# The prompt's probabilities turned by VectorE and SBUF copies instead of TensorE transposes, in a two-branch attention layer

## The reference

```python
def _dense_attn(q, k, v):
    s = jnp.einsum('bqhd,bkhd->bhqk', q, k).astype(jnp.float32) * ATTN_SCALE
    p = _softmax_f32(s).astype(v.dtype)
    o = jnp.einsum('bhqk,bkhd->bqhd', p, v)
    return o.reshape(q.shape[0], q.shape[1], -1)
```

## Time and profile before

| | us |
|---|---|
| time, median of 3 runs | 1204.24 |
| the three runs | 1206.59, 1204.24, 1203.47 |
| span of the profiled execution, first to last instruction | 1206.4 |
| TensorE matmul busy | 1182.1 (98%) |
| VectorE busy | 827.8 (69%) |
| ScalarE busy | 610.5 (51%) |
| 928 transposes at line 1165, 64 of them of the prompt | 124.7 busy |

### The profile page before, as it was taken

The page is one execution under the profiler, slowest core; times in us unless marked ns, Lnnn a source line. Parts: engine busy times, 40 slices in busy tenths (PEclk is TensorE's granted clock), DMA queues, the critical chain, the costliest instruction groups (busy, mean ns, idle before and its releaser), DMA issues.

```text
span 1206.4 us, 19639 instructions
## 1 busy us (share of the span) xinstructions
PE 1182.1 (98%) x7384; PEld 1080.7 (90%) x7384; DVE 827.8 (69%) x1621; ACT 610.5 (51%) x1224; POOL 97.0 (8%) x110
## 2 busy tenths in 40 slices
PE   7999999999999999999999999999999999999998
PEld 1899889989998999899899999989989988998996
DVE  6869458756766775687687697688679876354453
ACT  6742335534543554465465555556547675344342
POOL 0000200000000000000000000000000034533431
PEclk9999989999999999999999999999999999999999
DMA  9817612141122213221411111411023376642640
GB/s 360 307 52 227 226 35 68 47 138 46 57 83 93 65 40 103 81 72 65 144 64 40 55 58 46 112 62 58 22 60 120 119 237 204 214 149 91 208 141 35
DMA packets 71362, 132.81 MB, mean 110 GB/s; under 512 B 6758, under 2 KB 48102, under 8 KB 71276
## 3 DMA queue, kind: packets, MB, share of 16 engines
q1 hardware_dynamic: 57452, 109.70, 28.0%
q10 hardware_dynamic: 13824, 21.96, 5.0%
HBM read 96.24 MB, written 35.40 MB: 109 GB/s over the span
## 4 chain that ended last, share of the span: by engine, by line
PE 83%; DVE 8%; ACT 3%; DMA 2%; issue 2%; SPq 1%; POOL 0%; ACTq 0%; DVEq 0%
PE d_ps_pairs L94 23%; PE s_ps_pairs L94 11%; PE y_ps L2043 9%; PE o_ps_pairs L1195 9%; PE b_ps L94 9%; PE t_ps_pairs L1165 8%; PE v_ps L94 4%; PE s_ps_pairs L1129 4%; PE s_ps_pairs L1128 4%; DMA x<-in_w_ada 2%; PE k_ps L415 1%; DVE mn L1565 1%; DVE q L1550 1%; PE v_ps L429 1%; DVE pt L1559 1%
## 5 line engine op out<-in xcount | busy, mean ns | idle before, releaser
L94 PE MATMUL d_ps_pairs<-h,wt 128*128 128x384 f32 (+4 forms) x1848 | 352.1, 345 | 0.9 <-ACT craw L1358 0.9
L94 PEld LDWEIGHTS d_ps_pairs<-h,wt 128*128 128x128 f32 x1848 | 317.9, 188 | 14.7 <-ACT craw L1358 1.9
L1559 DVE TENSOR_TENSOR pt<-t_ps_pairs,pt 128x512 fp32r<-128x512 f32 (+2 forms) x264 | 153.0, 620 | 62.3 <-ACT pt L1313 60.8
L94 PE MATMUL s_ps_pairs<-h,wt 128*128 128x512 f32 (+1 forms) x864 | 174.7, 359 | 3.0 <-DVE q L1516 3.0
L94 PEld LDWEIGHTS s_ps_pairs<-h,wt 128*128 128x128 f32 x864 | 143.4, 191 | 25.2 <-DVE q L1516 3.2
L1313 ACT ACTIVATE pt<-t_ps_pairs 128x512 fp32r<-128x512 f32 (+2 forms) x264 | 130.2, 544 | 25.6 <-PE t_ps_pairs L1165 20.3
L1337 ACT ACTIVATE pr<-s_ps_pairs,mx 128x896 f32<-128x896 f32 (+1 forms) x128 | 124.9, 981 | 27.1 <-DVE mx L1587 26.8
L1165 PE MATMUL t_ps_pairs<-ident_sb,pr 128*128 128x128 f32 x928 | 124.7, 274 | 0.8 <-DVE pt L1559 0.3
L2043 PE MATMUL y_ps<-wo,mg 128*128 128x512 f32 (+1 forms) x504 | 113.2, 385 | 0.0
L1165 PEld LDWEIGHTS t_ps_pairs<-ident_sb,pr 128*128 128x128 f32 x928 | 105.6, 140 | 6.5 <-DVE pt L1559 3.1
L2043 PEld LDWEIGHTS y_ps<-wo,mg 128*128 128x128 f32 x504 | 91.4, 188 | 20.5
(11 more groups left out here) (217 smaller groups left out, 1618.4 us busy)
## 6 DMA issues: line engine op xcount, KB each, us to landing
wraw<-in_w_gate SPq DMA_DIRECT2D x24, 512.0 KB, 3.7
gt<-gates_d SPq DMA_DIRECT2D x40, 256.0 KB, 4.5
v_d<-vst SPq DMA_DIRECT2D x20, 320.0 KB, 4.6
wada<-in_w_ada SPq DMA_DIRECT2D x12, 512.0 KB, 7.1
gates_d<-craw ACTq DMA_DIRECT2D x30, 192.0 KB, 1.9
oz<-gates_d SPq DMA_DIRECT2D x20, 256.0 KB, 4.4
oz<-o_d SPq DMA_DIRECT2D x20, 256.0 KB, 4.1
x_f<-in_x SPq DMA_DIRECT2D x10, 512.0 KB, 6.5
```

The source lines that it names most:

```text
L94: mm = eng.matmul(out, lhs(a, k), rhs(b, k), start=(k == 0 and i == 0), stop=(k == n_k - 1 and i == 2))
L1559: dve.tensor_tensor(pt[:, 1, c * 512:c * 512 + cols], t_ps[:, n % 2, 0:cols], pt[:, 0, c * 512:c * 512 + cols].bitcast(F32), ALU.subtract) ...
```

## The change

In the prompt's step the probabilities are no longer turned by TensorE. VectorE, after the scaling, transposes each of the four 128x256 tiles in squares of 32 by 32 (four instructions), into a new tile `sq` in which squares that go to the same partitions lie together. SyncE then issues sixteen copies from SBUF to SBUF, of 32 partitions by 1 KB each, that bring row group i and column group j of the squares to their places in a new tile `qt`. ScalarE's high halves and VectorE's low halves of the prompt read `qt` where they read `t_ps`. The new waits: VectorE's squares for its own scalings; SyncE's copies for the squares (`sq_done`); ScalarE's high half for all copies (`qt_in`, 16 x 16 per pair); ScalarE's exponentials of step 1, which overwrite `pr`, for the squares. TensorE's eight transposes of the prompt and the wait for the scaling ahead of them are gone. Some semaphores of the two branches are merged to stay within their number, and memory is made for the new tiles.

```diff
@@ pairs: helpers
+    def prompt_squares(t, h):
+        if A:
+            return sq[:, :, :].rearrange("p j (h k t a) -> p h k t j a", h=2, k=2, t=2)[:, h, :, t]
+        return sq[:, :, :].rearrange("p j (k h t a) -> p k h t j a", h=2, k=2, t=2)[:, :, h, t]
+    def turned_prompt(c):
+        return qt[:, :, 4 * c * 32:4 * (c + 1) * 32].rearrange("p i (b a) -> p b i a", a=32)
@@ SyncE, behind the loads of the values
+            sp.wait_ge(sq_done, (pb + 1) * 4)
+            for i in range(4):
+                for j in range(4):
+                    sp.dma_start(qt[32 * j:32 * (j + 1), i, :], sq[32 * i:32 * (i + 1), j, :]).then_inc(qt_in, 16)
             load_tile(1)
@@ TensorE
-                if s > 0:
-                    for c in range(min(2, chunks[s - 1])):
+                if s > 1:
+                    for c in range(2):
                         transposes(s - 1, c)
@@ ScalarE, high
-                    act.wait_ge(t_done, chunk_base(p) + n + 1)
+                    if s == 0:
+                        act.wait_ge(qt_in, (pb + 1) * 256)
+                    else:
+                        act.wait_ge(t_done, turned_count(p, n + 1))
+                    if s == 0:
+                        act.activation(pt[:, 0, c * 512:c * 512 + cols].rearrange("p (b i a) -> p b i a", i=4, a=32),
+                                       turned_prompt(c), ACT.Copy).then_inc(hi_done, 1)
+                        continue
@@ ScalarE, exps
-                        act.wait_ge(t_done, chunk_base(p) + (chunk0[s - 1] + min(2, chunks[s - 1]) if s > 0 else 0))
+                        if s == 1:
+                            act.wait_ge(sq_done, (pb + 1) * 4)
+                        else:
+                            act.wait_ge(t_done, turned_count(p, chunk0[s - 1] + 2 if s > 0 else 0))
@@ VectorE, low
+                    if s == 0:
+                        part = lambda n: pt[:, n, c * 512:c * 512 + cols].rearrange("p (b i a) -> p b i a", i=4, a=32)
+                        dve.tensor_tensor(part(1), turned_prompt(c), part(0).bitcast(F32), ALU.subtract).then_inc(lo_done, 1)
+                        continue
@@ VectorE, normalise
+                if s == 0:
+                    for t, h in ((0, 0), (0, 1), (1, 0), (1, 1)):
+                        c = 2 * t + h
+                        scaled = dve.tensor_scalar(prompt_probs(t, h), prompt_probs(t, h), rden[:, c:c + 1], None, ALU.mult)
+                        if h == 1:
+                            scaled.then_inc(p_done, 1)
+                    dve.wait_ge(p_done, pb * 2 * STEPS + 2)
+                    for t, h in ((0, 0), (0, 1), (1, 0), (1, 1)):
+                        dve.transpose(prompt_squares(t, h),
+                                      prompt_probs(t, h).rearrange("p (k j b) -> p k j b", j=4, b=32)).then_inc(sq_done, 1)
+                    return
@@ kernel
-    nc = bacc.Bacc("TRN2", target_bir_lowering=False, num_devices=1)
+    nc = bacc.Bacc("TRN2", target_bir_lowering=False, num_devices=1, dynamic_dma_scratch_size=1024)
```

More of the change, by code:

```diff
@@ L842, in pairs @@
     s_ps, t_ps, o_ps, d_ps = (tiles[n] for n in ("s_ps", "t_ps", "o_ps", "d_ps"))
+    sq, qt = tiles["sq"], tiles["qt"]
     CH = 2 if A else 1
@@ L884, in pairs @@
     (craw_in, c_split, ckh, cvh, s_done, m_done, exp_done, r_done, p_done, t_done, hi_done, lo_done, pva_done,
-     pvb_done, ot_done, o_done, d_done, g_done) = (counts[n] for n in COUNTS)
+     pvb_done, ot_done, o_done, d_done, g_done, sq_done, qt_in,
+     proj_done, xa, xd, m1_done) = (counts[n] for n in COUNTS)
     g_out = [counts["g_out0"], counts["g_out1"]]
-    proj_done, xa, xd, x_used = sem("proj_done"), sem("xa"), sem("xd"), sem("x_used")
-    vw_in, m1_done, o_out = sem("vw_in"), sem("m1_done"), sem("o_out")
+    vw_in, o_out, x_used = sem("vw_in"), sem("o_out"), sem("x_used")
+    proj0, x0, m10 = (0, 0, 0) if A else (PAIRS * 6, PAIRS * 9, PAIRS * SAMPLES)
     if A:
@@ L919, in chunk_base, with turned_count @@
         return (0 if A else PAIRS * NCHUNK["a"]) + p * NCHUNK[branch]
+    def turned_count(p, n):
+        return chunk_base(p) + n - 2 * (p + base) - (2 if n >= 2 else 0)
+    def prompt_squares(t, h):
[4 more added lines that the diff above has]
+        return qt[:, :, 4 * c * 32:4 * (c + 1) * 32].rearrange("p i (b a) -> p b i a", a=32)
     def rows(ap, g):
@@ L1276, in projected @@
                 tok, bank = slice(t0, t0 + tn), s_ps[:, bank, 0:tn]
-                act.wait_ge(proj_done, p * NG + n + 1)
+                act.wait_ge(proj_done, proj0 + p * NG + n + 1)
                 if A and n < 3:
@@ L1367, in tile_high @@
                 else:
-                    sem, value = [(d_done, UNIT0[pb]), (proj_done, p * NG + 3), (d_done, UNIT0[pb] + ENDS[pb][0]),
+                    sem, value = [(d_done, UNIT0[pb]), (proj_done, proj0 + p * NG + 3), (d_done, UNIT0[pb] + ENDS[pb][0]),
                                   (d_done, UNIT0[pb] + ENDS[pb][1 if last else 2])][n]
@@ L1545, in projected @@
                         dve.tensor_copy(q1[HD:P, h, tok], rot[h * HD:(h + 1) * HD, 0:tn]).then_inc(xd, 1)
-                    dve.wait_ge(xa, p * 6 + 2 * n + 2)
-                    dve.wait_ge(xd, p * 6 + 2 * n + 2)
+                    dve.wait_ge(xa, x0 + p * 6 + 2 * n + 2)
+                    dve.wait_ge(xd, x0 + p * 6 + 2 * n + 2)
                     for h in range(2):
@@ L1573, in minima @@
                     dve.wait_ge(band_in, 16)
-                    dve.wait_ge(m1_done, p * STEPS + s + 1)
+                    dve.wait_ge(m1_done, m10 + p * STEPS + s + 1)
                     dve.tensor_tensor(nm[:, 0:2], mn[:, 0:2], nsk[:, :], ALU.min).then_inc(m3_done, 1)
@@ L1600, in prompt_minima @@
                 dve.tensor_reduce(grid4(mn), both, AX.X, ALU.min).then_inc(m1_done, 1)
-                dve.wait_ge(m1_done, p * STEPS + 1)
+                dve.wait_ge(m1_done, m10 + p * STEPS + 1)
                 dve.wait_ge(nsk_done, p + 2)
@@ L1619, in normalise @@
                 dve.wait_ge(r_done, pb * STEPS + s + 1)
-                for t in range(2):
[L1621 to L1627, removed]
+                if s == 0:
[9 more added lines that the diff above has]
+                    return
+                for t in range(2):
                     dve.tensor_scalar(probs_run(s, t), probs_run(s, t), rden[:, t:t + 1], None, ALU.mult
@@ L2155 @@
 COUNTS = ("craw_in", "c_split", "ckh", "cvh", "s_done", "m_done", "exp_done", "r_done", "p_done", "t_done",
-          "hi_done", "lo_done", "pva_done", "pvb_done", "ot_done", "o_done", "d_done", "g_done")
+          "hi_done", "lo_done", "pva_done", "pvb_done", "ot_done", "o_done", "d_done", "g_done", "sq_done", "qt_in",
+          "proj_done", "xa", "xd", "m1_done")
 TILES_TOTAL = 3 + 5 * PAIRS + 4 * PAIRS
 GAP0, GAP1, GAP2 = 896, 512, 344
+SPARE = 1792
 def build(nc, io):
@@ L2172, in build @@
     with ExitStack() as ctx:
+        turn = {n: sb(ctx, n, shape) for n, shape in (("sq", [P, 4, 8 * 32]), ("qt", [P, 4, 8 * 32]))}
+        sb(ctx, "spare", [P, SPARE])
         hm = sb(ctx, "h", [P, 2, KD, TOK], F32R)
@@ L2207, in build @@
             ("pr", [P, 2, NB + PAST + NB], F32), ("pt", [P, 2, 14 * P], F32R))}
+        tiles.update(turn)
         psum = ExitStack()
@@ L2222, in build @@
     with ExitStack() as ctx:
+        sb(ctx, "turned", [P, 4 * 4 * P + SPARE])
         wb = [wt[:, 0, :, :], wt[:, 1, :, :]] + [sb(ctx, f"wb{j}", [P, 2, D], F32R) for j in range(2, KD)]
```

## The result

The changed kernel takes 1266.79 us (median of 4 runs, 1265.07 to 1268.3), the kernel before in the same series 1204.80 (1203.47 to 1206.59): a ratio of 1.0513, interval 1.0497 to 1.0528. That is 62.0 us slower, where 36.4 had been forecast, and 4.8 us above the range. The direction held; the size is that of rival (b), whose rate of issue was the true one.

The account below looks back on a forecast made before the run. TensorE, busy 98%, was taken to bound the kernel, with VectorE and ScalarE on the chain in B. Delays of 14.4 us in A, 10 for A's clock and 12 in B made 36.4, so 1240.6 us; range 1216 to 1262.

Parts of the forecast that it names:

- rival (b): SyncE's queue backs up at a pitch of 0.60 to 0.70 us; at 0.65, 30 us more, 1270 us; chance 0.12.
- the pitch of SyncE's issues: Sixteen copies in a row on SyncE's queue: 0.40 us each, ends 0.28 and 0.70; last begins 6.0 us after first.
- The landing: Each SBUF-to-SBUF copy: 1.9 us from issue to landing, plus 0.1 for the semaphore.
- The path behind the landing: ScalarE's high halves await all copies, delaying step 1's exponentials and TensorE; in A TensorE stalls 4.1 us.
- the sum for a pair of A: Scores of step 2 start 3.6 us later per pair of branch A, TensorE's gain counted in; 14.4 us over four.
- The clock in A: TensorE's clock falls behind the stall in each pair of A, costing 2.5 us each, 10 us in all.
- Rival (a): The clock holds at 2.4 GHz in the pairs of A: 10 us less, 1230.6 us; chance 0.25.
- The clock in B: A clock fall in B would stretch TensorE to about VectorE's chain: nothing taken, at most 1 us per pair.
- case (c): Issues are cheap, copies land some 2 us behind squares: A gains 3.5, B loses 6, 1206.8 us; chance 0.05.
- Squares: VectorE's four 128x256 square transposes per pair: 1.5 us taken, between 1.1 and 2.9.
- The gain on TensorE: Eight transposes removed per pair: 0.87 us in each pair of A, 3.5 in all; nothing in B.
- case (d): Copies land inside unit 1, in A within 3.6 us of the squares: 7.0 us faster, 1197.2 us; chance 0.03.

Follow-up runs that it names:

- The experiment with eight forms: Changed kernel with a different form of SBUF-to-SBUF copy in each of the eight pairs, to read the issue pitch; one execution, 1249.36 us.
- Eight copies: Changed kernel with eight copies of 64 partitions per pair in place of sixteen of 32, same bytes; 1225.46 us, ratio 1.0169 to the kernel before.
- Two queues: Changed kernel with eight of the sixteen copies issued by SyncE and eight by ScalarE; 1251.07 us, ratio 1.0369 to the kernel before.
- By way of DRAM: Changed kernel with five DMAs per pair instead of sixteen copies: four writes to DRAM, one read back; 1238.19 us, ratio 1.0274 to the kernel before.
- the filler: Changed kernel with unused matmuls behind unit 1 (28 per pair of A, 14 of B) to fill TensorE's stall; 1262.95 us, ratio 1.0477.
- free copies: Changed kernel without the sixteen copies, the halves reading the squares where they lie; 1210.22 us, ratio 1.0041 to the kernel before.
- squares alone: Kernel before plus VectorE's four square transposes per pair, which nobody reads; TensorE's transposes stay, no copies; 1212.13 us, ratio 1.0058.
- the late reading by way of DRAM: Changed kernel with five DMAs through DRAM, and the prompt's halves and weighted sum moved behind step 1's weight split and transposes; 1235.93 us, ratio 1.0254.
- sixteen read late: Changed kernel with its sixteen copies, the prompt's halves and weighted sum moved behind step 1's weight split and transposes; 1252.12 us, ratio 1.0401.

## Why the prediction was wrong

**The step that failed** is the pitch of SyncE's issues: 0.40 us taken, 0.63 measured. It is fifteen pitches in each of eight pairs, 8 x 15 x 0.23 = 27.6 us. The landing, the wait of ScalarE for the last copy and the path behind it came as forecast; the last copy was issued too late. I had rows for two partitions (0.24), for 128 (0.46) and for strided ones (0.70), and placed 32 partitions between the first two by their number of rows. The experiment with eight forms shows that rows don't enter. None of those rows was a series of copies from SBUF to SBUF, and the dearest one, 0.70 (eight in a row, strided; 0.66 to 0.80 over the four pairs of A), I had set aside with "four times the rows". Rival (b) gave 1270 at 0.65; at 0.63 it gives 1268. It deserved far more than 0.12, and the range should have reached to it. (That the queue backs up, as (b) put it, isn't shown: the pitch is the same for 8 KB as for 128 KB.)

**The path behind the landing** was right. TensorE was to stand still for 4.1 us in A, and with the measured pitch for 4.1 + 3.45 = 7.55; it did for 7.62. With the measured pitch the sum for a pair of A is 3.6 + 3.45 = 7.05 us and the clock, for one of B 3.0 + 3.45 = 6.45; B measured 6.4 to 6.5. The three kernels that vary the data's arrival bear out A: 3.6 us less one for each us by which the data comes sooner than 8.0. Eight copies, with the clock held: 2.0 by the sum, 2.4 measured. Two queues: 2.9 and the clock, 5.5 measured. By way of DRAM: 4.1 and the clock, 5.6 measured.

**The clock in A** was right in its mechanism and somewhat too large: 2.5 us taken. What the sum leaves for it is 9.06 - 7.05 = 2.0 in the third pair (1.6 to 2.7 over the four), 2.6 with two queues and 1.5 by way of DRAM; the filler gives 1.4 to 1.9. Four times 0.5 is 2 us less than my sum. With both corrections: 36.4 + 27.6 - 2.0 = 62.0, which is the measured difference; that it fits to the tenth is luck, as the pairs of A differ among themselves by 1 us. Rival (a), that it holds, did not come.

**The clock in B** was taken at nothing. In the changed kernel this holds: the fall lies behind the 4.48 us stall in the second pair and inside unit 1 (6.00 us) in the third, and both intervals are longer by what the arrival of the data explains. With free copies or squares alone it costs 0.9 to 1.4 us, and my price for case (c), 6 us in B, was too low for that reason: 10.

**Squares**: 1.42 us for four, 1.5 taken. **Landing**: 1.9, 1.9 taken. **The gain on TensorE**: 0.87 us in each pair of A by the row, 0.8 to 0.9 in the run with free copies; in B nothing. **Faster**, case (d), asked for data 3.6 us behind the squares; with 6.4 the pair already lost 2.4. Its 1197.2 was out of reach at any pitch: with free copies, which come 0.7 us behind the squares, the kernel takes 1210.2, as B gains nothing from the transposes that go and pays for the squares.

The rule that I set against my rows in case (c), in the Trainium skill's "DMA: Bandwidth & Descriptors", Issuing engines are not separate DMA queues, is that the time to start a DMA is usually small beside the DMA itself. For one copy here it is a third, 0.63 us beside a landing of 1.9; for sixteen in a row it misleads, as 10.06 us of issuing stand beside one landing of 1.9. What the same section says of several engines, that starting DMAs on them at the same time saves the sequencer's time, the run with two queues bears out in A: the last of its issues ends 6.0 us behind the start of the first (404.17 - 398.20), instead of 10.06.

## What to carry to other kernels

Count the DMA instructions of a step and not only its bytes: in a row on one queue each costs its pitch, and everything that waits for the last one waits for all. Before a chain of small copies replaces compute, ask how far behind its producer the data may come (here 3.6 us in A, an estimate from the earlier trace rows), and divide that by the number of issues. Where such a price is not in the trace, the range must reach to the dearest row near it, and that end should not be cut by an argument (here the number of partitions) that no rows bear out. And read a run stretch by stretch before its total is held against a rival's: the total of the late reading by way of DRAM came near a rival's whose reason its intervals contradict.

## What the runs showed of the hardware

- A copy from SBUF to SBUF costs SyncE's queue 0.60 to 0.64 us when issued in a row, whatever its form (16 to 128 partitions, 8 to 128 KB). In three pairs of two runs (filler, sixteen read late) the same sixteen took 10.9 to 11.0 us, 0.68 to 0.69 each; why isn't known. Writes from SBUF to DRAM took 0.44 to 0.54. Two queues issued side by side at 0.62 and 0.67.
- Copies of 32 KB landed in 1.9 us, writes of 128 KB in 2.3, a read of 512 KB in 3.9.
- The clock's fall was not decided by a gap's length alone. It held behind stalls of 2.68 and 2.71 us and fell behind one of 2.48 in the same run (eight copies); it fell behind 2.15 (filler) and 1.9 (squares alone), and held behind 2.17 (DRAM, read late). In the second pair of B the same gap of 2.33 us ahead of unit 1 was followed by full clock in the changed kernel (24 matmuls in 4.43 us) and by a fall with free copies. What decides it was not found.
- In the third pair of A of the changed kernel the fall of the clock cost TensorE 1.1 us in the weighted sum and 1.2 in the scores of step 2, of which 2.0 us, by the sum, reached the length of the pair. In the second pair of B a weighted sum of 2.04 us added nothing that shows: the interval is 6.5 us longer, and the data's arrival explains 6.45.
